# Index scores of a hybrid decoder layer: sums from VectorE to ScalarE and GpSimd, and a new order of the second half of the mixers

## The reference

```python
# delta rule: t_inv is the inverse of a unit lower triangle, one for each head and chunk
u = jnp.einsum('bhncs,bhnse->bhnce', t_inv, v_beta)
w = jnp.einsum('bhncs,bhnsd->bhncd', t_inv, k_beta * jnp.exp(g)[..., None])
def step(state, xs):                      # once for each of 8 chunks
    v_new = u_c - jnp.einsum('bhcd,bhde->bhce', w_c, state)
    o_c = (jnp.einsum('bhcd,bhde->bhce', q_c * jnp.exp(g_c)[..., None], state)
           + jnp.einsum('bhcs,bhse->bhce', a_c, v_new))
    state = (state * jnp.exp(g_last)[..., None]
             + jnp.einsum('bhcd,bhce->bhde', k_c * jnp.exp(g_last - g_c)[..., None], v_new))
# sparse attention: the index scores of a block of 128 queries, and its 128 best keys
idx_logits = jnp.einsum('bthd,bsd->bths', qi_b.astype(F32), k_idx)      # 16 index heads of 64
score = jnp.einsum('bths,bth->bts', jax.nn.relu(idx_logits), wi_b)
score = jnp.where(causal[None], score, -jnp.inf)
_, sel = lax.top_k(score, topk)
```

## Time and profile before

| | us |
|---|---|
| three runs | 1674.65, 1675.01, 1678.58 |
| median | 1675.01 |
| profiled execution | 1676.34 |
| its span in the profile | 1674.6 |
| TensorE busy | 1592.2 (95%) |
| VectorE busy | 1334.1 (80%) |
| ScalarE busy | 681.1 (41%) |
| GpSimd busy | 538.1 (32%) |

### The profile page before, as it was taken

The page is one execution under the profiler, slowest core; times in us unless marked ns, Lnnn a source line. Parts: engine busy times, 40 slices in busy tenths (PEclk is TensorE's granted clock), DMA queues, the critical chain, the costliest instruction groups (busy, mean ns, idle before and its releaser), DMA issues.

```text
span 1674.6 us, 26801 instructions
## 1 busy us (share of the span) xinstructions
PE 1592.2 (95%) x9303; PEld 1380.6 (82%) x9303; DVE 1334.1 (80%) x2453; ACT 681.1 (41%) x1070; POOL 538.1 (32%) x383
## 2 busy tenths in 40 slices
PE   7998887968999999999999999999999999999998
PEld 5876675536778999999999999998888888888886
DVE  6744588876732699999999999847889888888887
ACT  5574233254422343443354444433333333333334
POOL 2000000014510577888732333313333333322220
PEclk9999998979999999999999999999999999999999
DMA  4321010001233478888889999999999999999995
GB/s 142 101 85 39 2 40 1 26 27 50 88 95 144 139 208 286 286 281 281 259 290 365 340 348 345 343 316 407 387 381 384 392 385 376 387 369 349 354 362 199
DMA packets 148993, 404.47 MB, mean 242 GB/s; under 512 B 14085, under 2 KB 71685, under 8 KB 145449
## 3 DMA queue, kind: packets, MB, share of 16 engines
q1 hardware_dynamic: 108584, 243.92, 42.9%
q0 software_dynamic: 36864, 134.23, 20.9%
q10 hardware_dynamic: 3456, 25.17, 3.7%
HBM read 350.83 MB, written 52.44 MB: 241 GB/s over the span
## 4 chain that ended last, share of the span: by engine, by line
PE 55%; DVE 10%; issue 1%; DMA 1%; ACT 1%; POOL 0%; DVEq 0%; ACTq 0%
PE bank L1562 10%; PE bank L1560 10%; PE bank L1561 10%; PE bank L2078 7%; PE bank L2082 7%; PE bank L2079 7%; DVE own_waste L1863 3%; PE bank L2102 3%; DVE back L1914 1%; DMA h<-u_rows_dram,own_experts 1%; DVE rt_num L1885 1%; DVE rt_num L1878 1%; DVE rt_work L1879 1%; PE bank L2063 0%; DVE rt_cand L1897 0%
## 5 line engine op out<-in xcount | busy, mean ns | idle before, releaser
L2078 PE MATMUL bank<-hi_parts,rt_u_parts 128*128 128x384 f32 x1024 | 350.9, 343 | 0.0
L2079 PE MATMUL bank<-lo_parts,rt_u_parts 128*128 128x384 f32 x1024 | 343.7, 336 | 0.0
L1560 PE MATMUL bank<-rt_u_parts,rt_w_hi 128*128 128x512 f32 x768 | 299.0, 389 | 0.0
L1561 PE MATMUL bank<-rt_u_parts,rt_w_lo 128*128 128x512 f32 x768 | 298.8, 389 | 0.0
L1562 PE MATMUL bank<-rt_u_parts,rt_w_hi 128*128 128x512 f32 x768 | 298.8, 389 | 0.0
L1778 ACT ACTIVATE rt_u_parts<-raw 128x1024 fp32r<-128x1024 f32 x126 | 133.8, 1062 | 337.5 <-PE bank L2082 302.3
L1420 ACT ACTIVATE rt_u_parts<-raw 128x1024 fp32r<-128x1024 f32 x128 | 135.9, 1061 | 322.0 <-PE bank L1562 294.5
L2131 POOL DMA_INDIRECT h<-u_rows_dram,own_experts x128 | 172.7, 1349 | 236.3 <-DVE own_waste L1863 222.3
L2137 POOL DMA_INDIRECT qy<-v_dram,own_experts x128 | 131.3, 1026 | 346.9 <-DVE qy L1494 341.0
L1476 DVE TENSOR_TENSOR rt_u_parts<-raw,rt_u_parts 128x1024 fp32r<-128x1024 f32 x128 | 156.6, 1223 | 70.0 <-ACT rt_u_parts L1420 68.0
L1825 POOL TENSOR_TENSOR rt_u_parts<-raw,rt_u_parts 128x1024 fp32r<-128x1024 f32 x66 | 162.8, 2466 | 127.6 <-ACT rt_u_parts L1778 126.3
(11 more groups left out here) (356 smaller groups left out, 2568.1 us busy)
## 6 DMA issues: line engine op xcount, KB each, us to landing
raw<-u_dram SPq DMA_DIRECT2D x128, 512.0 KB
raw<-v_dram SPq DMA_DIRECT2D x128, 512.0 KB
active_scratch<-rt_act SPq DMA_DIRECT2D x128, 192.0 KB
gates_scratch<-front ACTq DMA_DIRECT2D x12, 1024.0 KB
gates_scratch<-back ACTq DMA_DIRECT2D x12, 1024.0 KB
front<-gates_scratch SPq DMA_DIRECT2D x8, 1536.0 KB
front<-active_scratch SPq DMA_DIRECT2D x64, 192.0 KB
back<-active_scratch SPq DMA_DIRECT2D x64, 192.0 KB
```

Source lines behind the costliest of these rows:

```text
L1560: mm(bank, w_hi[:, j, block], v_hi[:, j, cols], start=False, stop=False)
L1561: mm(bank, w_lo[:, j, block], v_hi[:, j, cols], start=False, stop=False)
L2078: mm(bank, u_hi[:, j % 2, chunk[c]], hi[:, c, 0:TD], start=c == 0, stop=False)
L2079: mm(bank, u_hi[:, j % 2, chunk[c]], lo[:, c, 0:TD], start=False, stop=False)
```

## The change

- The sums leave VectorE. ScalarE, after rectifying two products, multiplies each in place by its head's weight (`weigh`, an activation with a scale for each partition), and GpSimd adds the weighted rows up (`accumulate` in its block). For each block GpSimd does 15 additions.
- Block 2's index products, with their rectifiers and weightings, stand beside levels 3 and 4, as block 1's do beside levels 1 and 2. Only block 3's are left in the chunks: four in each of chunks 0 to 3, in two pairs, and all index products use banks 2 and 3.
- The 12 up-projections stand in chunks 0 to 6 (1, 2, 2, 2, 2, 2, 1), the keys' four first, on banks 0 and 1.
- The rounds of selection are set anew: 12 of block 1 in the levels (10 before), then 4, 5, 5, 5, 4, 4, 4 and 5 in the chunks.
- The load of `w_q_up` waits for the 32nd sum instead of the 16th.

```diff
@@ -602,22 +602,24 @@
-    LEVEL_SUMS = {(1, 3): range(0, 4), (2, 1): range(4, 8), (2, 3): range(8, 12), (3, 1): range(12, 16)}
+    UPS = (1, 3, 5, 7, 0, 2, 4, 6, 8, 9, 10, 11)
+    CHUNK_UPS = (range(0, 1), range(1, 3), range(3, 5), range(5, 7), range(7, 9), range(9, 11), range(11, 12), range(0))
+    LEVEL_BEST = {(3, 3): (1, 0, 2), (4, 1): (1, 2, 4), (4, 3): (1, 4, 7), (5, 1): (1, 7, 9), (5, 3): (1, 9, 12)}
...
@@ -692,7 +694,7 @@
-                sp.wait_ge(s["score"], IH)
+                sp.wait_ge(s["score"], 2 * IH)
                 sp.dma_start(wq, a_in["w_q_up"]).then_inc(s["wq"], 16)
@@ -708,7 +710,19 @@
+                def accumulate(q):
+                    b, i = of_block(q)
+                    S = (b + 1) * P
+                    pool.wait_ge(s["weighed"], q + 1)
+                    if i > 1:
+                        pool.wait_ge(s["score"], q)
+                    first = relu_row(q - 1) if i == 1 else score[b]
+                    nc.gpsimd.tensor_tensor(score[b][:, 0:S], first[:, 0:S], relu_row(q)[:, 0:S],
+                                            ALU.add).then_inc(s["score"], 2 if i == 1 else 1)
                 for b in range(1, NB):
+                    for q in range((b - 1) * IH + 1, b * IH):
+                        accumulate(q)
                     pool.wait_ge(s["score"], b * IH)
@@ -890,9 +889,6 @@
-                        if n < 4:
-                            for q in range(IH + 8 * n + 4 * part, IH + 8 * n + 4 * part + 4):
-                                accumulate(q)
                         take_best(*CHUNK_BEST[n][part])
@@ -939,22 +935,37 @@
+                def weigh(q):
+                    b, i = of_block(q)
+                    S = (b + 1) * P
+                    act.wait_ge(s["relu"], q + 1)
+                    if q == 0:
+                        act.wait_ge(s["w_idx"], 1)
+                    a(relu_row(q)[:, 0:S], relu_row(q)[:, 0:S], ACT.Copy, scale=w_idx[:, b, i:i + 1]).then_inc(s["weighed"], 1)
+                def weighted(first, end):
+                    for q in range(first, end, 2):
+                        rectify(q)
+                        rectify(q + 1)
+                        weigh(q)
+                        weigh(q + 1)
@@ -1000,21 +1011,16 @@
-                    if level < 3:
-                        for q in range(8 * level - 8, 8 * level):
-                            rectify(q)
+                    if level < 5:
+                        weighted(8 * level - 8, 8 * level)
@@ -1168,13 +1172,9 @@
-                    if q >= IH:
-                        pe.wait_ge(s["relu"], max(IH, q - 3))
-                        bank = t.bank[q % 4]
...
+                    if q >= 2:
+                        pe.wait_ge(s["relu"], q - 1)
+                    bank = t.bank[2 + q % 2]
@@ -1226,7 +1226,7 @@
-                        if level < 3 and h % 2:
+                        if level < 5 and h % 2:
@@ -1272,12 +1270,15 @@
-                        for q in range(IH + 8 * n + 4, IH + 8 * n + 8):
+                        for q in range(2 * IH + 4 * n, 2 * IH + 4 * n + 2):
                             index_dots(q)
...
+                    if n < 4:
+                        for q in range(2 * IH + 4 * n + 2, 2 * IH + 4 * n + 4):
+                            index_dots(q)
@@ -1288,16 +1289,8 @@
-                    if n < 3:
-                        for q in range(IH + 8 * n + 8, IH + 8 * n + 12):
-                            index_dots(q)
...
+                    for k in CHUNK_UPS[n]:
+                        up_project(NIDX + k)
```

More of the change, by code:

```diff
@@ L673, in relu_row @@
         def relu_row(q):
[L674 removed]
+            if q < 2 * IH:
                 return conv[:, H + q % 6, :] if q % 6 < H else row(4 + q % 6)
@@ L864, in _ @@
                         tt_(pair[:, h, both], pair[:, h, both], t.bank[4 + h][:, both], ALU.subtract).then_inc(s["level"], 1)
-                        for q in LEVEL_SUMS.get((level, h), ()):
-                            accumulate(q)
                         if (level, h) in LEVEL_BEST:
@@ L941, in take_up @@
                     act.wait_ge(s["up"], n + 1)
-                    m = n - NIDX
-                    if m < 0:
+                    if n < NIDX:
                         dest, bank = up_idx[n], t.bank[6 + n % 2]
                     else:
-                        dest, bank = (up_q, up_k)[m % 2][:, m // 2, :] if m < 2 * H else vt[:, m - 2 * H, :], t.bank[m % 4]
+                        m = UPS[n - NIDX]
+                        dest, bank = (up_q, up_k)[m % 2][:, m // 2, :] if m < 2 * H else vt[:, m - 2 * H, :], t.bank[n % 2]
                     a(dest, bank[:], ACT.Copy).then_inc(s["up_out"], 1)
@@ L1010, in _ @@
                     ins.then_inc(s["w"], 1)
-                for q in range(IH, IH + 4):
-                    rectify(q)
                 for n in range(NCH):
                     if n < 4:
-                        for q in range(IH + 8 * n + 4, IH + 8 * n + 8):
-                            rectify(q)
+                        weighted(2 * IH + 4 * n, 2 * IH + 4 * n + 4)
                     else:
@@ L1024, in _ @@
                       t.bank[5][:, 0:H * CHUNK].rearrange("p (h c) -> p h c", h=H), ACT.Copy).then_inc(s["o_copy"], 1)
-                    if n < 3:
-                        for q in range(IH + 8 * n + 8, IH + 8 * n + 12):
-                            rectify(q)
-                    elif n < 7:
-                        for m in range(3 * n - 9, 3 * n - 6):
-                            take_up(NIDX + m)
+                    for k in CHUNK_UPS[n]:
+                        take_up(NIDX + k)
                 act.wait_ge(s["o_copy"], NCH)
@@ L1144, in up_project @@
                     else:
-                        if m < 4:
-                            pe.wait_ge(s["relu"], 3 * IH)
-                        else:
-                            pe.wait_ge(s["up_out"], n - 3)
-                        bank = t.bank[m % 4]
+                        if n == NIDX:
+                            pe.wait_ge(s["wkv"], 16)
+                            pe.wait_ge(s["latents"], 4)
+                        if n == NIDX + H:
+                            pe.wait_ge(s["wq"], 16)
+                        pe.wait_ge(s["up_out"], n - 1)
+                        bank = t.bank[n % 2]
                     for c in range(2):
@@ L1170, in index_dots @@
                         pe.wait_ge(s["qk"], H)
-                    if q >= IH:
-                        pe.wait_ge(s["relu"], max(IH, q - 3))
-                        bank = t.bank[q % 4]
-                    else:
-                        if q >= 2:
-                            pe.wait_ge(s["relu"], q - 1)
-                        bank = t.bank[2 + q % 2]
+                    if q >= 2:
+                        pe.wait_ge(s["relu"], q - 1)
+                    bank = t.bank[2 + q % 2]
                     rows = slice(IDIM * (i % 2), IDIM * (i % 2) + IDIM)
@@ L1290, in _ @@
                     last.then_inc(s["out"], 1)
-                    if n < 3:
-                        for q in range(IH + 8 * n + 8, IH + 8 * n + 12):
-                            index_dots(q)
-                    elif n < 7:
-                        if n == 3:
-                            pe.wait_ge(s["wq"], 16)
-                            pe.wait_ge(s["wkv"], 16)
-                            pe.wait_ge(s["latents"], 4)
-                        for m in range(3 * n - 9, 3 * n - 6):
-                            up_project(NIDX + m)
+                    for k in CHUNK_UPS[n]:
+                        up_project(NIDX + k)
                 def logits(u):
```

29 lines of the change are left out of this document (7 added, 22 removed).

## The result

| | before | after |
|---|---|---|
| median (7 runs each, one chip) | 1675.24 us | 1680.98 us |
| lowest to highest | 1674.65 to 1678.58 | 1678.51 to 1682.30 |
| profiled execution, span | 1676.34, 1674.6 | 1681.83, 1679.9 |
| mean granted clock of it | 0.983 | 0.980 |

A forecast was written before the change was run, and what follows sets the result against it. VectorE's sums and selection were taken to bound the chunks, up to chunk 7's start at L883. Levels +11.7, dropped products -1.5 and chunks -18.9 gave -8.7 us, so 1666.3 us, range 1660 to 1674.

The forecast's parts named there:

- the last of the levels: Selection after level 5: three rounds instead of two ahead of L872, one round of 0.97 us, of which 0.9 shows.
- The forecast of -8.7: Whole change: levels +11.7, products ahead of chunk 0 -1.5, chunks -18.9 us; chance 0.50 within 1662 to 1671.
- clock rival: Chunks bound by TensorE: low-clock dips, 3.5 us each, no longer hidden by VectorE; five cost 17.5, 1684 us; chance 0.08.
- sum of the levels: Levels, with block 2's index products, trailing weightings, vanished waits and one more selection round: together +11.7 us.
- trailing weightings: Levels 2 to 5: last two weightings delay ScalarE's copies, TensorE waits 0.5 us in 2 and 3, 0.85 in 4 and 5: 2.7.
- cheap-levels rival: Levels: products and weightings hide in waits TensorE has anyway; some 5 us more gain, 1661 us; chance 0.17.
- The chunks: Chunk 0 to L883 of chunk 7: TensorE bounds chunks 1 to 5, sum 67.9 us, 18.9 less than before.
- lock rival: Levels and chunks: VectorE's two-operand SBUF instructions and GpSimd's additions exclude each other; +6 us, 1672; chance 0.15.
- the rival by which the gain is given back there: Behind the mixers the gain is given back, or an unseen wait keeps chunks from shortening; 1675 us; chance 0.10.

The follow-up runs named there:

- two rounds: The changed kernel with two rounds of selection ahead of the copies of u instead of three, one more in chunk 0; 1670.66 us, ratio 0.9969.
- copies first: The changed kernel with the three rounds of selection ahead of the copies of u moved behind them into chunk 0; 1670.76 us, ratio 0.9961.
- sums alone: The kernel before with only the sums moved to ScalarE and GpSimd, order of products, up-projections and selection kept; 1666.48 us, ratio 0.9929.
- filler: The changed kernel with two unused 128x512 products put into TensorE's wait ahead of the third u product; 1678.79 us, ratio 1.0009.
- before copies late: The kernel before with four rounds of selection instead of two ahead of the copies of u; 1682.47 us, ratio 1.0049.
- copies ahead: Copies first, with the last two weightings of a level moved behind the first two `xs` copies of the next; 1666.79 us, ratio 0.9939.
- sums alone with the gap filled: Sums alone, with two index products (chunks 0 to 3) or the flip (4 to 7) put into each chunk's wait; 1663.82 us, ratio 0.9915.
- after again: The changed kernel measured again without alteration, against the kernel before; 1680.35 us, ratio 1.0017.
- order alone: Copies first with the sums back on VectorE, so the new order stands without the relief; 1689.80 us, ratio 1.0082.

## Why the prediction was wrong

**The term that failed is the last of the levels:** "Selection after level 5 has three rounds instead of two ahead of L872, one round of 0.97, of which 0.9 shows." The round's own price was right: 1.83 against 0.85 us with two rounds. Two things were left out. First, the wait grew from nearly nothing (0.1 us before at 246.10) to 1.83, not by 0.9. Before, TensorE stands for 1.06 us in level 5's last products, for which the trace names nothing; that wait is in no term of the sum, and it is gone after. So TensorE's first u product comes 1.6 us ahead of VectorE's last subtraction (251.41 and 253.00), and before it came 0.8 ahead (241.90 and 242.68). Rows of before:

```profile
241.61 0.50 PE L1227 MATMUL bank<-qy,front 64*64 64x64 f32 x9 [1.06 <-issue]
...
246.10 1.09 PE L1244 MATMUL bank<-conv,qy 64*64 64x128 f32 x16
```

Second, a wait of that length was priced by its length alone. Behind it the clock was low, where before it was high:

| where | after | at full pace, in two rounds | lost |
|---|---|---|---|
| third u product to chunk 0 | 8.21 | 4.99 | 3.2 |
| chunk 0 | 15.35 | 269.32 - 260.34 = 8.98 | 6.4 |
| chunk 5 | 10.91 | 322.51 - 313.26 = 9.25 | 1.7 |

Together 11.3 us, 9.6 of them behind the wait. The forecast of -8.7 and these 11.3 make +2.6. From level 2 to chunk 7 the traces have +4.1. The missing 1.5 are 1.0 up to the third u product (the wait is 0.9 longer than its term) and 0.5 in the chunks. Chunk 7 starts 2.7 us later, close to the 2.6, but that is luck: the 2.7 holds the 1.2 us of level 1.

**The clock rival, with its chance of 0.08, was the right mechanism.** It was sought in the chunks alone ("the new chunks hold only waits of about 1 us"), which was true and beside the point: the long wait stood ahead of them. Its price was taken from the one stretch behind chunk 5, 3.5 us lost; this one cost 9.6 (3.2 + 6.4). The trace of before had more of them than the one priced: the granted clock is 0.63 from 264 to 268 us and 0.50 from 288 to 292, at waits of 3.32 and 5.37 us. And the cover was thinner, as the text had seen: before, such stretches lay in part under VectorE's work.

**The sum of the levels was near.** Level 2 took 10.97 us from its first product to level 3's (about 10.9 summed), level 3 12.25 (11.7), level 4 12.67 (12.1), level 5 5.12 (6.2). The waits for ScalarE's trailing weightings were 0.72, 0.72, 1.15 and 1.15, 3.7 instead of 2.7, and the 1.06 us wait of before that no term had is gone. The two errors cancel, which is luck. The cheap-levels rival falls.

**The chunks were right but for the clock.** Chunks 1, 2, 3 took 10.61, 10.69, 10.38 against 10.45, chunk 4 9.23 against 9.23, chunk 6 to `vnew` of chunk 7 9.3 against 9.4, chunk 0 at full pace 8.98 against 8.7. TensorE bounds them. (Where the prediction says of VectorE that "its up-projections now begin in chunk 0", they are TensorE's.) From chunk 0 to chunk 7 the sum was 67.9 and the trace has 76.5, the difference being 6.4 and 1.7 of clock and 0.5 of rest.

**What remains without the wait** is -6.1 us (copies first) or -6.0 (two rounds) on the medians, not -8.7. In both traces a slow stretch stands in chunk 4 (308 to 316 us, and 304 on), where chunk 4 takes 12.56 instead of 9.23: 3.3 us. From level 2 to chunk 7 these traces have -5.3 and -5.1; without the 3.3 it would be -8.6 and -8.4. So at full clock the rest of the sum holds to about 1 us. Why the clock falls in chunk 4 there and in chunk 5 of after is not shown.

**The lock rival falls as a bound.** GpSimd's additions took 1.27 us at 512 columns, so 1.04 was no bound for them, 1.02 at 384 and 0.73 at 256. Groups of after from 200 to 345 us, by form (busy us, mean ns, idle):

```profile
L853 DVE TENSOR_TENSOR raw<-hi,cst 128x256 f32<-128x256 f32 x19 | 11.1, 616 | 6.0 <-PE bank L1217 5.9
...
L762 DVE MAX8 gdn_best<-proj 128x8 f32<-128x384 f32 x16 | 9.0, 561 | 0.5
...
L885 DVE TENSOR_TENSOR lo<-lo,gdn_ghalf 128x512 f32<-128x512 f32 x8 | 5.5, 684 | 0.1
```

The masks, which read two operands in SBUF, take 616 ns on average against 422 before. The decays in the chunks of after keep their price (684 ns, 685 before); in sums alone one took 1.51 us instead of 0.68 (261.51 above), beside two additions that began 0.03 us ahead of it. So VectorE does stand for a GpSimd addition now and then, as the Trainium skill, "SBUF — State Buffer", section "Who interferes with whom", says, and as the prediction read from the earlier trace rows. MAX8 (559 before) is untouched. In sum it is 19 x 0.19 = 3.7 us of VectorE, in levels where VectorE waits for TensorE (5.9 us at this line). By the warning that moving work between the two might not help, which the prediction cites from the Trainium skill, "Perfetto Trace Analysis", section "Optimizing Scalar/DVE Operations", the time would have been the lock rival's 1672; the move alone gave 1666.5 and is the half that gains.

**The end moves with chunk 7:** before and after, the first probability follows its start by 16.0 us (15.4 to 18.6 in the other traces), so for this change the rival by which the gain is given back there falls.

## What to carry to other kernels

Relieving the engine that bounds a stretch uncovers the next one: then every wait of TensorE on the new path is to be listed, those ahead of the stretch too, and one of about 2 us priced with the half-pace stretch that may follow it (here 9.6 us behind 1.83). Fill such waits with products that the program has anyway. Such a wait need not bring the stretch every time, so its price is a chance and a size. And measure the parts of a change apart: moving the sums gained 10.9 us alone, and the new order beside it gave back 4.8 of them, or all and more with three rounds ahead of the copies.

## What the hardware showed

- **The slow clock outlasted the idle time by far.** From 270 to 280 us TensorE of after was busy without a gap, at half pace:

```profile
270.00:280.00 10.00, 10.00 (x31) 5.89 (x29) 3.72 (x11) 4.88 (x9) 3.69 (x3) 0.50 0.00 1
```

  The low stretch was 23.6 us in both executions of after; the one in chunk 4 of copies first was about 6.7 us, by its loss of 3.3. The Trainium skill, "TensorE: Matmul & The Clock Gate", section "What's actually happening", says that the default is the slow clock and that activity releases it. This window is against it as far as activity is TensorE's busy time in the trace. What ends a slow stretch is not settled here.
- **The same wait does not always bring it.** Ahead of level 1's first product TensorE waits 1.98 us in all 13 traces. In seven of them the granted clock is below full in level 1 (before, copies first, filler, before copies late, sums alone, copies ahead, sums alone with the gap filled), in six it is not. At the third u product, waits of 1.83, 1.83 and 2.10 us brought it (after, after again, before copies late), and one of 2.12 did not (order alone). The windows of 198 to 206 us, first of before, then of after again:

```profile
198.00:206.00 8.00, 6.02 (x144) 5.79 (x138) 4.92 (x12) 2.90 (x7) 0.00 (x0) 0.79 0.01 2
```

```profile
198.00:206.00 8.00, 6.55 (x164) 5.67 (x166) 4.68 (x11) 4.04 (x12) 0.59 (x1) 1.00 0.01 2
```

  So a kernel's time carries a chance part, and the range of one kernel's runs (8 us in after again) is wider than the 0.3% named ahead. That is why the medians of 4 to 10 runs are compared here and not two profiles. Where slow stretches fall in chunks 4 to 7 stays open.
